# Decoder step on one core: an opening in another order, late weights prepared in a written-out first tile, and four tiles per turn of the second loop

## The reference

```python
def memory_kv(mem, g, w, k_gain):
    k, v = jnp.split(rms_norm(mem, g) @ w, [MEM_W], axis=-1)
    k = rms_norm(k.reshape(B, M, MEM_HEADS, HEAD_DIM), k_gain)
    return k, v.reshape(B, M, MEM_HEADS, HEAD_DIM)

def forward(...):
    for i in range(N_A_LAYERS):                      # one pooling layer
        z = rms_norm(x, norm_a[i]) @ w_in_a[i]
        u, gp, qm, gm = jnp.split(z, [POOL_W, 2 * POOL_W, 2 * POOL_W + MEM_W], axis=-1)
        yp = pool_mixer(u_ext, pos, pool_mix_w[i], pool_scale[i]) * jax.nn.silu(gp)
        ym = memory_branch(qm, gm, mem_q_norm[i], mem_k[i], mem_v[i])
        x = x + jnp.concatenate([yp, ym], axis=-1) @ w_out_a[i]
    k, v = jnp.split(rms_norm(x, kv_norm) @ w_kv, [KV_W], axis=-1)
    for j in range(N_B_LAYERS):                      # one window-attention layer
        z = rms_norm(x, norm_b[j]) @ w_in_b[j]
        q, gq, qm, gm = jnp.split(z, [SWA_W, 2 * SWA_W, 2 * SWA_W + MEM_W], axis=-1)
        ys = swa_banded(q, k, v, sinks[j]) * jax.nn.silu(gq)
        ym = memory_branch(qm, gm, mem_q_norm[li], mem_k[li], mem_v[li])
        x = x + jnp.concatenate([ys, ym], axis=-1) @ w_out_b[j]
```

## Time and profile before

| | us |
|---|---|
| median of 3 runs | 1635.84 |
| lowest, highest | 1631.94, 1636.43 |
| the profiled execution | 1638.76 |
| its span, first to last instruction | 1637.0 |
| TensorE busy in the span | 1525.4 (93%) |
| VectorE, ScalarE, GpSimd busy | 845.8, 546.6, 508.6 |

### The profile page before, as it was taken

One profiled execution on the slowest core, in us unless ns is written; L12 is line 12 of the kernel. 1 busy time (PEld: TensorE's weight loads), 2 busy tenths in 40 slices (PEclk: granted clock), 3 DMA queues, 4 the chain that ended last, 5 costly groups with the idle time before them and its releaser, 6 DMA issues.

```text
span 1637.0 us, 32475 instructions
## 1 busy us (share of the span) xinstructions
PE 1525.4 (93%) x12861; PEld 1176.0 (72%) x12861; DVE 845.8 (52%) x1772; ACT 546.6 (33%) x1351; POOL 508.6 (31%) x365
## 2 busy tenths in 40 slices
PE   5847999999999999989999999999999999999996
PEld 3626888888888888875775767757577576675774
DVE  3757555545555554534553635536356373563753
ACT  2352332423233242322432514325143251432522
POOL 0114353434435343431423304233042331423310
PEclk9878999999999999999999999999999999999996
DMA  9032122212212221277200010000100101001050
GB/s 399 15 137 103 66 107 101 104 65 91 92 65 107 101 104 65 90 299 297 103 27 27 2 53 1 24 30 1 53 1 3 50 1 53 1 1 52 1 189 28
DMA packets 25121, 127.38 MB, mean 78 GB/s; under 512 B 2455, under 2 KB 3095, under 8 KB 12518
## 3 DMA queue, kind: packets, MB, share of 16 engines
q1 hardware_dynamic: 24830, 124.88, 19.7%
q10 hardware_dynamic: 144, 0.37, 0.1%
HBM read 87.64 MB, written 39.74 MB: 78 GB/s over the span
## 4 chain that ended last, share of the span: by engine, by line
issue 52%; POOL 26%; PE 11%; DVE 5%; ACT 2%; DMA 1%; POOLq 1%; SPq 0%; ACTq 0%; DVEq 0%
PE ps_z L694 5%; POOL tiny_sb L2413 5%; POOL ph_sb L2544 3%; POOL pm_sb L2456 3%; POOL pm_sb L2438 2%; POOL big_sb L2419 2%; POOL w_x_sb L2445 2%; POOL ph_sb L2505 2%; POOL ph_sb L2503 1%; POOL ph_sb L2509 1%; POOL big_sb L2421 1%; DVE xn_sb L1681 1%; PE ps_t L637 1%; PE ps_z L708 1%; DMA x_buf_sb<-x 1%
## 5 line engine op out<-in xcount | busy, mean ns | idle before, releaser
L671 PE MATMUL ps_z<-xn_sb,w_in_sb 128*128 128x256 f16 (+1 forms) x4752 | 505.6, 265 | 9.8 <-DVE pm_sb L1721 9.2
L671 PEld LDWEIGHTS ps_z<-xn_sb,w_in_sb 128*128 128x128 f16 x4752 | 425.7, 98 | 76.7 <-issue 19.6
L694 PE MATMUL ps_z<-pm_sb,w_out_sb 128*128 128x256 f16 x3072 | 345.9, 273 | 0.0
L694 PEld LDWEIGHTS ps_z<-pm_sb,w_out_sb 128*128 128x128 f16 x3072 | 299.1, 98 | 38.5 <-issue 4.4
L2413 POOL TENSOR_TENSOR tiny_sb<-tiny_sb 128x8 f32<-128x8 f32 (+5 forms) x73 | 106.9, 1465 | 570.8 <-DVE tiny_sb L1727 281.8
L660 PE MATMUL ps_z<-w_in_sb,xn_sb 128*128 128x512 f16 (+1 forms) x792 | 171.2, 376 | 0.0
L1240 ACT ACTIVATE scr_sb<-ps_z,tiny_sb 128x256 f32<-128x256 f32 (+2 forms) x92 | 41.8, 491 | 368.2 <-PE ps_z L660 277.3
L1718 DVE TENSOR_REDUCE tiny_sb<-scr_sb 128x8 f32<-128x512 f32 (+2 forms) x62 | 36.6, 591 | 205.7 <-ACT scr_sb L1240 131.2
L660 PEld LDWEIGHTS ps_z<-w_in_sb,xn_sb 128*128 128x128 f16 (+1 forms) x792 | 77.7, 98 | 89.0 <-issue 0.2
L1801 DVE SCALAR_TENSOR_TENSOR x_buf_sb<-ps_z,tiny_sb,x_buf_sb 128x512 f32<-128x512 f32 x64 | 48.0, 751 | 118.4 <-PE ps_z L694 118.4
L2544 POOL TENSOR_TENSOR ph_sb<-ph_sb,tiny_sb 128x512 f32<-128x512 f32 x48 | 53.2, 1107 | 161.1 <-DVE tiny_sb L2172 161.1
(11 more groups left out here) (330 smaller groups left out, 2127.0 us busy)
## 6 DMA issues: line engine op xcount, KB each, us to landing
x_buf_sb<-x SPq DMA_DIRECT2D x18, 1024.0 KB, 4.9
w_x_sb<-w_b SPq DMA_DIRECT2D x18, 1024.0 KB, 5.8
x<-x_buf_sb SPq DMA_DIRECT2D x9, 1024.0 KB, 4.1
y<-x_buf_sb SPq DMA_DIRECT2D x9, 1024.0 KB, 3.9
parts<-ph_sb SPq DMA_DIRECT2D x16, 512.0 KB, 3.0
parts<-w_x_sb SPq DMA_DIRECT2D x16, 512.0 KB, 3.4
w_in_sb<-parts SPq DMA_DIRECT2D x8, 1024.0 KB, 9.5
w_out_sb<-w_mem SPq DMA_DIRECT2D x4, 1024.0 KB, 18.7
```

The source lines that it names most:

```text
L671: last = mm(ps_z[:, b, half * NT:half * NT + n], w_split[:, g, ws, kc, half * P:(half + 1) * P], xs[:, x, kc, 0:n], start=(kc == 0 and ws ...
L694: done = mm(ps_z[:, b, half * NT:(half + 1) * NT], w_out_split[:, g, ws, kc, half * P:(half + 1) * P], gated_parts[:, x, kc, :], start=sta ...
```

## The change

*The opening.* The mix and the transposed weights are loaded first, then the small inputs and the memory, and the eight mixed weights are TensorE's first work. `PREP` and `BATCHES` are new: the query group and the three mixed or pooling groups come first; there are five batches.

*Scales.* For the eight input groups ScalarE writes squares in bf16 (`squared`), TensorE sums them over the partitions with a matrix of ones (`column_sums`, 8 matmuls of 256 columns for each group), and DVE takes the largest column sum (`column_tops`, a reduction that reads PSUM). `rows_top` is gone. The output groups keep `batch_totals`.

*Square sums.* In the opening GpSimd adds the eight chunks of squares first (`sums`), as in the tiles, and TensorE needs one chunk.

*A first tile of its own.* Tiles 0 and 1 of loop A stand written out ahead of the loop, which turns three times. In tile 0 (`first=True`) the preparation of groups 7 to 12 is written between the steps of the tile, on all engines, and so are the second layer's key transposes. `T` has its own order of uses for that tile. The raw group 12 is loaded into `x_buf[:, 1]`, so the load of the second tile of x waits for its low part.

*Loop B* has four tiles in a turn, `Fori(0, TILES // 4)`.

```diff
-PREP = [None, 0, 4, 5, 6, 7, 1, 2, 3]
-BATCHES = [(1, 3), (3, 6), (6, 7), (7, 9), (9, 11), (11, 15)]
+PREP = [None, 0, 4, 1, 2, 3, 5, 7, 6]
+BATCHES = [(1, 4), (4, 7), (7, 9), (9, 11), (11, 15)]
...
+            def column_sums(name, groups):
+                T.wait_free(pe, part_of(name), 0, name)
+                for i, j in enumerate(groups):
+                    pe.wait_ge(top_sum.sem, top_sum.after("pre", 0, j - 1))
+                    for kc in range(KC):
+                        last = mm(ps_t[:, i * 256:(i + 1) * 256], ones_half, squared[j][:, kc, :],
...
+            def column_power(i):
+                a, b = BATCHES[i]
+                if b - a == 3:
+                    column_tops(f"top{i}a", a, a + 2).then_inc(T.free[0], 1)
+                    T.wait_read(dve, "pre", 0, f"top{i}a")
+                    a += 2
+                own(column_tops(f"top{i}", a, b))
...
+                if first:
+                    column_sums("top2", (7, 8))
+                    memory_keys(1)
+                    split_in(3)
                 split_features("A", t, "u0", 1)
+                if first:
+                    batch_totals(3)
+                    split_in(4)
...
+            pooling_tile(0, True)
+            pooling_tile(1, False)
+            with pe.Fori(0, TILES // 2 - 1) as it:
                 for p in range(2):
+                    pooling_tile(it * 2 + (2 + p), False)
...
+                if first:
+                    memory_keys(1)
+                    end(7)
+                    end(8)
+                    act.wait_ge(u_free.sem, u_free.after("A", t, -1))
+                    pooled_inputs(0)
+                    start(11)
+                    start(12)
+                    memory_tops()
+                    pooled_inputs(1)
+                    end(9)
+                    end(10)
+                    pooled_inputs(2)
+                    queries()
+                    end(11)
+                    end(12)
+                    next_squares()
+                    mem_exps("A", t, 0)
...
+                if first:
+                    queries()
+                    batch_power(2)
+                    batch_power(3)
+                    gained(t, 0)
+                    batch_power(4)
+                    gained(t, 1)
...
-            with pe.Fori(0, TILES // 2) as it:
-                for p in range(2):
-                    t = it * 2 + p
+            with pe.Fori(0, TILES // 4) as it:
+                for q in range(4):
+                    t, p = it * 4 + q, q % 2
```

More of the change, by code:

```diff
@@ L1981, in window_differences, with pooling_tile, row_top_in, queries @@
                 ve.tensor_copy(u[:, :, 0:16], u[:, :, NT:UW]).then_inc(u_free.sem, 1)
[L1983 to L1992 removed]
+            def pooling_tile(t, p, first):
+                def row_top_in(s):
+                    dve.wait_ge(w_gained.sem, w_gained.after("A", t, s))
+                    row_top_of("A", t, s, row_tops[:, s, :], stages[s])
+                def queries():
@@ new lines, in pooling_tile @@
+                own.wait()
+                own(tt(win_b[:, 4:6, 16:UW], win_a[:, 4:6, 16:UW], win_a[:, 4:6, 8:UW - 8], ALU.add))
+                own.wait()
+                tt(win_b[0:HD, 4, 16:UW], win_a[0:HD, 4, 16:UW], ones[0:HD, 0:1].to_broadcast([HD, NT]), ALU.mult).then_inc(win_sums.sem, 1)
+                sums("A", t, 0)
+                rstd(T, "A", t, "ss")
+            pooling_tile(0, True)
+            pooling_tile(1, False)
+            own.loop(9)
+            with pool.Fori(0, TILES // 2 - 1) as it:
+                for p in range(2):
+                    own.tile(it * 2 + p)
+                    pooling_tile(it * 2 + (2 + p), False)
@@ L2546, in _ @@
             own.loop(8)
[L2547 to L2549 removed]
+            with pool.Fori(0, TILES // 4) as it:
+                for q in range(4):
+                    t, p = it * 4 + q, q % 2
                     own.tile(t)
```

765 lines of the change are left out of this document (404 added, 361 removed).

## The result

| | before | after |
|---|---|---|
| median, us | 1636.13 | 1611.22 |
| lowest, highest | 1631.94, 1637.2 | 1610.78, 1612.4 |
| the profiled execution | 1638.76 | 1610.78 |
| its span | 1637.0 | 1609.0 |
| first tile's first matmul | 120.24 | 79.33 |

The ratio of the times is 0.985 (interval 0.9837 to 0.987): 25 us less. The last four rows come from TensorE's timelines of the two profiled executions, whose times differ by 28.0, and divide that: -40.9 at the start of the first tile, +19.7 in it, -1.7 from there to the second loop, -4.5 to its last tile, -0.6 behind it. About half of what the opening gains is paid for in the first tile.

What follows compares the result with a forecast made beforehand. TensorE was taken to bound the loops, with gains left in opening, first tile and back edges: -23.8 - 1.8 - 4.1 = -29.7 from 1638.76 gives 1609.1, less 2.9 to the median, 1606; range 1588 to 1621.

Steps and rivals of the forecast that it cites:

- The sum: Whole kernel: -29.7 us in total, 1609.1 for the profiled execution, less 2.9 to the median: 1606.
- Start of the first tile, 77.2: Opening: TensorE's and DVE's chains both end near 77, so the first tile starts at 77.2 instead of 120.24, -43.0.
- The collision at 47: Opening: DVE's low part of weight group 2 waits for GpSimd's additions until 51.5 and ends at 53.8.
- the diagonal: Opening: TensorE waits 2.6 us for the diagonal behind the held low part.
- First tile, 103.5: First tile: DVE, ACT and GpSimd set its end; 103.5 instead of 84.23, +19.3; second tile starts at 180.7.
- The port: Opening and first tile: DVE and GpSimd share an exclusive SBUF port pair; priced so, the first tile ends about 181.
- Its two ends without collisions: First tile's end: about 178 if nothing collided, 172.5 without any blocking and slow restart.
- The cover: First tile: ScalarE and DVE keep pace, TensorE's waits vanish, second tile starts at 148; 1574 us; chance 0.09.
- The longer chain: First tile: all six low parts are blocked, +12, second tile at 193; 1618 us, 1626 with slow hand-overs; chance 0.11.
- The low clock: First tile: TensorE runs it all at 1.2 GHz, end at 219, with waits 232; 1644 to 1658 us; chance 0.05.
- the third rival: First tile: TensorE's clock stays low, 1644 to 1658 us, chance 0.05; most of its cases were put in 1588 to 1621.
- The edges, -1.8 and -4.1: Loop back edges: pooling loop has two waits instead of three, -1.8; window loop goes from 3 edges to 1, -4.1.

Runs made afterwards that it cites:

- the run with the query copy first: The kernel after with ScalarE's copy of the last pooling inputs and queries ahead of the high part of group 10 in the first tile: 1614.53 us.
- low 9 first: The kernel after with VectorE's low part of weight group 9 ahead of the first slot row maximum in the first tile: 1611.01 us.

## Why the prediction held, and where its sizes were off

- *The sum.* The prediction set 1609.1 for the profiled execution; it took 1610.78. The 5 us between 1606 and the median of 1611.22 are mostly the 2.9 subtracted to get from one execution to the median. That step was wrong, for it took the profile after to be as slow an execution as the profile before. The profile of before held a restart at the lower clock, 1.7 us, and a second profile of the same program (1639.09) held two; the profile of after held none at its edges and lies 0.4 under its median.
- *Start of the first tile, 77.2: it was 79.33.* The mixed groups ran from 10.26 with one wait of 1.33, where none over 1 was forecast: it was for the two scalings beside GpSimd's first addition. The next matmuls stood at 36.27 instead of 35.5; in five other profiles with this opening the scalings came first, took 0.48, and those matmuls stood at 34.1 to 34.6. The collision at 47 was forecast with the wrong turn-taking: low 2 was to wait for all three additions, and these were to run at full speed. In fact the two engines took turns by instruction; the additions lost 3.7 us and the low part 2.1. Their end at 54.3 instead of 51.5 held up TensorE by 3.99 us instead of 1.9, and the second column sums then ran slowly (3.59 for 16 matmuls, against 1.91 for the first 16; granted clock 0.56 at 54.3 to 60). Against that, the 2.6 us set for the diagonal did not come: TensorE had no wait there. The 2.1 us are thus what is left of larger errors of both signs, and that they nearly cancel is luck. On VectorE's side the steps named from 60.2 on add up to 74.3 (with the hand-overs of 0.06 each, under 75) and not to 76.9. That both engines arrive together held: at 79.33 TensorE had waited 0.26 for VectorE.
- *First tile, 103.5: it was 103.9.* Here the mechanism held, step by step. The chain through four engines set the end, not the matmuls: low 12 ended 53.8 us behind the tile's start (54.7 in the prediction), the third gate began at 65.0 (64.8), and the rest took 38.9 (38.65). The four waits came to 3.4, 6.4, 4.0 and 7.3 where 3.8, 5.9, 3.9 and 6.1 were forecast; a wait of 1.3 ahead of the last totals was not. That a step in the chain can give way only to show the next was seen in the run with the query copy first. Of the six groups only four were ready at 120 in before: the low parts of 11 and 12 ended at 136.4, within the old first tile and ahead of the queries for which TensorE waited 9.21 us there.
- *The port.* By the Trainium skill, "SBUF — State Buffer", section "SBUF: two separate sides", the pair of ports that the two engines share goes for a whole instruction to whichever starts first, a GpSimd instruction or a VectorE instruction that has two SBUF inputs or runs in a mode that uses two ports. The collisions above agree in the taking of turns: an instruction that was held up ends with the other engine's, or one instruction of its own length behind it. Which mode the scale steps run in, no run here shows. The prediction applied the rule to the large low parts; the small scale steps, which it took at 2.6 us with their totals and power, lost 3.4 in after at one step and 7.3 with low 9 first, where low 2 lost 2.1.
- *Its two ends without collisions.* 172.5, there without the slow restart as well, follows from its terms: 180.7 less 5.1 us of blocking and 2.5 of restart is 173.1. 178 does not follow: with the restart that sum is 175.6. No run was without collisions, so neither is tested.
- *Rivals.* The cover did not hold: 23.7 us were idle in the first tile. The longer chain: low 10 took 4.96 us, but the other five of the six took 2.3 each. The low clock: it did fall at each of the four waits, with 0.77, 0.65, 0.50 and 0.60 granted over the matmuls right behind them, and cost some 6 us of matmul time in sum (16 matmuls of the scores took 3.78 where 2.00 is their time in a run without that wait). It was back at 1.00 within the work that followed, but for the transposes between the last two waits, and all but the last of these losses lie ahead of a further wait for another engine. Behind the last, 24 matmuls took 4.57 instead of 2.78: 1.8 lost, where the prediction set 2.5. Where the prediction puts most of the third rival's cases in its range, its own numbers fit the second (1618) and not the third (1644 to 1658).
- *The edges, -1.8 and -4.1: they were -0.9 and -4.5.* In the pooling loop two edges of 2.29 and 2.17 remained where the mean of before, 1.8, was taken. In the window loop the idle time fell by 3.9, and a restart of 1.7, which the prediction didn't price, went with two edges. Against that the tiles took 0.16 us more than in before, 1.1 for seven; 0.13 of it stayed with two tiles per turn, so it is mostly not the longer turn, and its cause is open.

## What to carry to other kernels

Work moved out of an opening into a first tile cost here what the longest chain through the engines costs, so look there for steps without a near reader (here weight halves) and write them behind those that the bound engine waits for. Where VectorE and GpSimd work side by side, look for the smallest instructions that grew, and move the GpSimd work beside VectorE steps that keep their time (here those that read PSUM) rather than only elsewhere. Price a loop's back edge with its idle time and the slow matmuls behind it, and judge a change of 2 us by a mark in its own stage.

## What the runs showed of the hardware

- VectorE instructions on two to four numbers per partition, 0.15 to 0.28 us alone, took 1.85 to 3.56 beside a GpSimd instruction, ending with it. Which condition an instruction must meet to be held up was not tried; the reductions of 2.28 us kept their time beside the same work (2.27 at 123.65 in after, beside the window sums), and so did eight multiplications that read PSUM (3.21 us).
- The same opening ran in two ways because of this: where the two scalings at 19 us started ahead of GpSimd's first addition they took 0.48 us, where one started beside it 2.64, and the first column sums then stood some 2 us later.
- After an idle time of about 2 us at a loop's back edge TensorE ran the next matmuls in part at the lower clock in some turns and not in others: 12.22 or 10.53 us for the same 48, behind waits of 2.12 us in both cases. In the eleven profiles that have such edges it did so behind 9 of 41.
- A loop whose one turn holds all eight tiles took 0.13 us more per tile than the same kernel in turns of two (101.74, 101.61), and saved 1.6 to 2.3 us for each jump left out, besides the restarts.
